# Squares of the delta stage's queries and keys split into high and low parts, two units at a time

## The chip, the cores and the metric

The kernel runs on one core of a Trainium2 chip. The metric is device time in microseconds (us) of one execution, as the median of several runs; a profile is one further execution with the hardware profiler on. TensorE (PE) multiplies matrices, VectorE (DVE) and ScalarE (ACT) work elementwise, GpSimd (POOL) makes constants and issues some loads, SyncE (SP) issues the weight loads.

## The reference

Two layers of a decoder on 256 tokens of 2048 features, all in float32. Layer 0 mixes with a short convolution and a gated DeltaNet of 8 heads, layer 1 with sparse attention; each is followed by a SwiGLU network. The change touches only the norms of queries and keys in the DeltaNet part:

```python
def l2norm(t):
    return t * lax.rsqrt(jnp.sum(jnp.square(t), axis=-1, keepdims=True) + NORM_EPS)

    qkv = jax.nn.silu(causal_depthwise_conv(dn_qkv, dn_conv_w))
    q, k, v = jnp.split(qkv, 3, axis=-1)
    q, k, v, z = l2norm(heads(q)), l2norm(heads(k)), heads(v), heads(dn_z)
```

## The kernel before

**Weights and matmuls.** Every large product is made of three fp32r matmuls on parts: each weight half (128 x 1024 elements, 512 KB) is split into `w_hi`, a rounded copy made by ScalarE (line 681), and `w_lo`, the rest, made by VectorE (line 1192). TensorE multiplies high by high, high by low and low by high (`passes`, lines 1935 to 1937). The parts lie in four slots (`HL_SLOTS`): ScalarE may write half h only when TensorE has used half h - 4 (`half_used`); VectorE follows on `w_hi_ready`, TensorE on `w_lo_ready`. A chunk is eight halves: 512 output columns over all 2048 inputs. In the stage in question the output is by feature, and a half is 24 matmuls of 256 columns. SyncE loads the weights, four slabs of two halves ahead.

**Order.** Each engine runs its own program in order; the order is written out by hand. `halves(n)` in the program of ScalarE or VectorE makes the next n weight parts, so the place of other work among them is fixed.

**The stage around the change.** The six chunks of the short convolution (`sc`, lines 2184 to 2191) run on TensorE while the other engines finish queries, keys and values of the DeltaNet part in `qkvT`. In turn m = 1 to 4 (one per chunk) two units of queries or keys are normalised, eight units in all, each 128 features by 512 values (two heads). ScalarE squares a unit (`square`, line 853), TensorE multiplies the squares by a matrix of ones (`squares_sum`, line 2174), which puts the sum on all partitions, ScalarE takes the root (`norm`, line 860) and VectorE divides (`unit`, lines 1482 and 1483). TensorE's sums stand behind the third half of the chunk for the first unit (2m - 2) and behind the sixth for the second (2m - 1). ScalarE's order in a turn is: square, four halves, root, square, three halves, root, one half, and then the SiLU of the next four heads. VectorE's is: five halves, unit, three halves, unit. Between turns 1 and 2 VectorE multiplies two chunks (line 1503) and runs a convolution (`conv`, lines 1445 and 1447, with one half inside it); turn 2 then starts with four halves instead of five (line 1508). Between turns 2 and 3 stands line 1532, between turns 3 and 4 nothing, and after turn 4 again line 1503 and a convolution, then the decays, whose cumulated sums go out to memory and come back by a broadcast load before the DeltaNet's chunk matrices can be made (line 1541). `norm_sq`, the buffer of the squares, exists once, and so does `norm_q`, that of the roots.

Of the kernel before, what the change touches and what calls it, by code (L numbers as in the profile page):

```python
# [13 lines left out]
F32 = mybir.dt.float32  # L14
F32R = mybir.dt.float32r
I32 = mybir.dt.int32
ALU = mybir.AluOpType
ACT = mybir.ActivationFunctionType
# [3 lines left out]
P = 128  # L22
# [56 lines left out]
def trunk(nc, x_in, positions, ln_mix_g, ln_mix_b, ln_ffn_g, ln_ffn_b, ffn_w_in, ffn_w_out,  # L79
          hy_w_in, sc_conv_w, dn_conv_w, dn_a_log, dn_dt_bias, dn_norm_w, hy_w_out,  # L80
          nsa_w_in, cmp_pos_k, cmp_w1_k, cmp_w2_k, cmp_pos_v, cmp_w1_v, cmp_w2_v, nsa_w_out,
          inv_freq, ln_by_feature, end_positions, x_by_feature, gc_rows, beta_rows, out, stop=None):
# [3 lines left out]
    with ctx:  # L86
        def sem(name):
            return ctx.enter_context(nc.semaphore(name))
# [3 lines left out]
        def sb(name, shape, dt=F32, offset=None):  # L92

            size = 4 * int(np.prod(shape[1:]))
            if offset is None:
                offset = place[0]
                place[0] += (size + 31) // 32 * 32
            return nc.alloc_sbuf_tensor_at(name, shape, dt, offset=offset)
# [13 lines left out]
        big_at = place[0]  # L112
        big = sb("big", [P, 12288])
        yt_at = place[0]
        yt = sb("yt", [P, KT, SEQ])
        gb_at = place[0]
        gb = sb("gb", [P, 2, D])
        ident = sb("ident", [P, P])
        ones = sb("ones", [P, P])
        upper = sb("upper", [P, P])  # L120
        neg_lower = sb("neg_lower", [P, P])
        blk_mask = sb("blk_mask", [P, len(BLOCKS), P])
# [25 lines left out]
        qkvT = part(24 * SEQ, "p (f t) -> p f t", f=24)  # L148
# [35 lines left out]
        conv_in = gb_flat[:, 0:2048].rearrange("p (a f t) -> p a f t", a=2, f=4)  # L184
        conv_out = gb_flat[:, 2048:3072].rearrange("p (f t) -> p f t", f=4)
        ba_out = yt[:, KT - 1, :]
        norm_sq, norm_q = (gb_flat[:, n:n + 512].rearrange("p (h d) -> p h d", h=4) for n in (3072, 3584))

        hT = big[:, 0:FT * SEQ].rearrange("p (f t) -> p f t", f=FT)
        yt_flat = yt[:, :, :].rearrange("p a t -> p (a t)")  # L190
# [67 lines left out]
        gb_in, out_done = sem("gb_in"), sem("out_done")  # L258
        consts, pool_chain, x_scaled = sem("consts"), sem("pool_chain"), sem("x_scaled")
        dve, act_done = sem("dve"), sem("act_done")  # L260
        var_ready, std_ready, nmr_ready, x_normed = sem("var_ready"), sem("std_ready"), sem("nmr_ready"), sem("x_normed")
        xt_hi_ready, xt_lo_ready = sem("xt_hi_ready"), sem("xt_lo_ready")
        stage_free, silu_done = sem("stage_free"), sem("silu_done")
# [105 lines left out]
        for (name, kts), slots in zip(OUTER, SPARES):  # L369
            for p, k in enumerate(slots):  # L370
                if k is not None:
                    h = 2 * (S[name] + kts) - 2 * TAIL + p
# [287 lines left out]
        def _(act):  # L660
            h_next = [0]

            def halves(count, i=None, per=0):

                for _ in range(count):
                    h = h_next[0]
                    if h >= 2 * total_slabs:
                        return
                    if h < 2 * RAW_SLOTS:
                        act.wait_ge((slab_in if h % 2 else first_in)[h // 2], 16)  # L670
                    elif h % 2 == 0:
                        act.wait_ge(slab_in[h // 2 % RAW_SLOTS], at(16 * (h // 2 // RAW_SLOTS + 1), i, 2 * per))
                    if before_in_slot[h] is not None:
                        act.wait_ge(half_used, at(before_in_slot[h] + 1, i, per))
                    if h in all_split:
                        act.wait_ge(a_lo_ready, all_split[h])
                    if h in gates_halves:
                        src = half_of(h).rearrange("p (k n) -> p k n", n=P)[:, :, P - N_GATES:]
                        act.activation(gates_of(h)[:, :, 0:N_GATES], src, ACT.Copy).then_inc(w_hi_ready, 1)
                    else:  # L680
                        act.activation(weights_of(h)[0], half_of(h), ACT.Copy).then_inc(w_hi_ready, 1)  # L681
                    h_next[0] += 1
# [167 lines left out]
                ins.then_inc(from_act, 1)  # L850

            def square(u):
                act.activation(norm_sq, qkvT[:, 2 * u:2 * u + 2, :].rearrange("p f (a t) -> p (f a) t", a=2),
                               ACT.Square).then_inc(act_done, 1)

            def norm(u):
                wait_sp(act, ("norm", u))
# [3 lines left out]
                               ACT.Sqrt, bias=eps_nm[:, :]).then_inc(sp_free[K[("norm", u)] % 4], 1)  # L861

            act.wait_ge(consts, 3)
            soft, expA = sm[:, 9, :], misc_w[:, 120:128]
            for j in range(2):
                for n in range(3):
                    m = 3 * j + n
                    if m == 0:
                        halves(8)
                        wait_sp(act, ("ba",))  # L870
                        act.activation(sm[:, 0:NT, :], last_cols(("ba",), 2 * DNH), ACT.Copy).then_inc(sp_free[K[("ba",)] % 4], 1)
                        done(act.activation(beta_feature, ba_out[P - 32:P, :], ACT.Sigmoid))
                        wait_sp_read(act, ("ba",))
                        done(act.activation(sm[:, 2, :].rearrange("p (t h) -> p t h", t=NT), sm[:, 0:2, 0:8], ACT.Sigmoid))
                    elif m < 5:
                        act.wait_ge(silu_done, m)
                        square(2 * m - 2)
                        halves(4)
                        norm(2 * m - 2)
                        square(2 * m - 1)  # L880
                        halves(3)
                        norm(2 * m - 1)
                        halves(1)
                    else:
                        halves(3)
                        act.wait_ge(for_act, 9)
                        done(act.activation(soft, sm[:, 8, :], ACT.Exp, scale=-1.0))
                        act.wait_ge(from_act, n_from[0])
                        done(act.activation(soft, soft, ACT.Ln, bias=1.0))
                        done(act.activation(expA, expA, ACT.Exp))  # L890
                        halves(3)
                    if n == 0:
                        c = C["sc"] + 3 * j
                        b = chunk_in(c)
                        act.wait_ge(stage_free, 7 + j)
                        for a in range(2):
                            ins = act.activation(conv_in[:, j, 2 * a:2 * a + 2, :],
                                                 b[a][:, :].rearrange("p (f t) -> p f t", f=2), ACT.Copy)
                        ins.then_inc(pair_free[c % 2], 1)

                    act.wait_ge(stage_free, m + 3)
                    act.activation(qkvT[:, 4 * m:4 * m + 4, :], qkvT[:, 4 * m:4 * m + 4, :], ACT.Silu).then_inc(silu_done, 1)
                    if m == 5:
                        act.wait_ge(for_act, 10)
                        done(act.activation(sm[:, 6, :], sm[:, 4, :], ACT.Exp))
                        done(act.activation(sm[:, 14, 8:16], sm[:, 14, 8:16], ACT.Exp))
                        halves(2)
# [159 lines left out]
            name = ("vcmp",)  # L1067
# [80 lines left out]
            v = x[:, 0, FIRST:]  # L1148
# [5 lines left out]
        def _(dv):  # L1154
# [25 lines left out]
            def halves(count, i=None, per=0):  # L1180

                for _ in range(count):
                    h = h_next[0]
                    if h >= 2 * total_slabs:
                        return
                    hi, lo = weights_of(h)
                    src = half_of(h)
                    if h in gates_halves:
                        src = src.rearrange("p (k n) -> p k n", n=P)[:, :, P - N_GATES:]
                        hi, lo = (gates_of(h)[:, :, n * N_GATES:(n + 1) * N_GATES] for n in range(2))  # L1190
                    dv.wait_ge(w_hi_ready, at(h + 1, i, per))
                    dv.tensor_tensor(lo, src, hi.bitcast(F32), ALU.subtract).then_inc(w_lo_ready, 1)  # L1192
                    h_next[0] += 1
# [233 lines left out]
            for p in range(8):  # L1427
                v = slice(2 * p, 2 * p + 2)
# [47 lines left out]
            def unit(u):  # L1476
# [5 lines left out]
                own(dv.reciprocal(r, r))  # L1482
                to_act(dv.scalar_tensor_tensor(v, r, SCALE if u < 4 else 1.0, v, ALU.mult, ALU.mult))

            def halves_and_units(m, first=5):

                halves(first)
                unit(2 * m - 2)
                halves(3)
                unit(2 * m - 1)  # L1490

            for j in range(2):
# [7 lines left out]
                b = chunk_in(c + 1)  # L1500
                for a in range(2):
                    v = conv_in[:, j, 2 * a:2 * a + 2, :].rearrange("p f t -> p (f t)")
# [6 lines left out]
                else:  # L1509
# [8 lines left out]
                    name = ("gc",)  # L1518
                    wait_sp(dv, name)
                    b = sp_bank(name)  # L1520
# [8 lines left out]
                b = chunk_in(c + 2)  # L1529
# [7 lines left out]
            for t, hh in units:  # L1537
                Dt = tiles_of(t, hh)[0]
                for h in range(4):
                    n = 8 * t + 4 * hh + h  # L1540
# [218 lines left out]
            name = ("kcmp",)  # L1759
# [153 lines left out]
        def _(pe):  # L1913
# [9 lines left out]
            def sp_done(ins, name):  # L1923
                ins.then_inc(sp_ready[K[name] % 4], 1)
# [243 lines left out]
            small(S["ba"], C["ba"])  # L2168

            def squares_sum(u):  # L2170
                pe.wait_ge(act_done, u + 1)
                name = ("norm", u)
                b = sp_use(name)
                sp_done(pe.matmul(b[:, :], ones[:, :], norm_sq.rearrange("p h d -> p (h d)"), start=True, stop=True), name)  # L2174

            def decays():

# [385 lines left out]
```

## Time and profile before

| | |
|---|---|
| median of three runs | 2379.5 us (2379.26 to 2380.42) |
| profiled execution | 2381.16 us, of which the span from the first to the last instruction is 2379.4 us |
| TensorE busy | 2345.6 us (99% of the span) |
| VectorE busy | 1558.2 us (65%) |
| ScalarE busy | 1123.7 us (47%) |
| line 2174 (the sums) | 16 matmul records, 592 ns each, two for each of eight units, 185.7 to 269.8 us |
| mean granted TensorE clock | 0.997 of full speed |

Times in the trace are us from the start of the span. A busy TensorE is not TensorE at its peak: matmuls overlap, so what counts is the distance from one start to the next.

### The profile page before, as it was taken

Reading aid. Unit: us, or ns where it says so; the run is one execution under the profiler, and the core shown is the slowest. Engines: PE = TensorE matmul, PEld = TensorE weight load, DVE = VectorE, ACT = ScalarE, POOL = GpSimd, SP = SyncE. Lnnn points to the kernel's source line nnn. Section 1 sums busy time; section 2 is a strip of 40 time slices with the busy share of each in tenths; the row PEclk is TensorE's granted clock in tenths of the full one; section 3 lists DMA queues with packets and bytes.
Section 4 is the critical chain, followed back from the end, with each engine's and each line's share of the span. In section 5 each row is a group of like instructions: output and inputs, shape, how many; then the busy total and the mean of one; then the engine's idle time right before and its main releaser. Section 6 shows DMA issues by size and latency. Waiting matters only on the chain.

```text
span 2379.4 us, 31884 instructions
## 1 busy us (share of the span) xinstructions
PE 2345.6 (99%) x12225; PEld 2008.2 (84%) x12225; DVE 1558.2 (65%) x2097; ACT 1123.7 (47%) x1516; POOL 34.6 (1%) x79
## 2 busy tenths in 40 slices
PE   8999999999999999999999999999999999999998
PEld 8999988888888888888889888888888888888886
DVE  6767776676666666755588657657666666666556
ACT  4346654654444444444465445546444444444443
POOL 1000000100000000000000000000000000000001
PEclk9999999999999999999999999999999999999999
DMA  7555441745555555655547643245555555565553
GB/s 268 184 188 185 166 146 64 300 152 194 193 195 194 194 189 194 227 192 192 192 173 236 227 145 107 89 160 195 177 195 194 194 194 194 194 217 204 191 191 115
DMA packets 180441, 440.08 MB, mean 185 GB/s; under 512 B 7304, under 2 KB 19728, under 8 KB 166016
## 3 DMA queue, kind: packets, MB, share of 16 engines
q1 hardware_dynamic: 177984, 425.75, 51.3%
q0 software_dynamic: 2368, 13.13, 1.4%
q8 instruction: 58, 0.95, 0.2%
q14 instruction: 31, 0.25, 0.0%
HBM read 436.74 MB, written 2.11 MB: 184 GB/s over the span
## 4 chain that ended last, share of the span: by engine, by line
PE 92%; DVE 3%; ACT 3%; issue 1%; DMA 1%; ACTq 0%; DVEq 0%
PE bank L1935 29%; PE bank L1937 29%; PE bank L1936 29%; PE bank L2228 2%; DVE w_lo L1192 1%; PE bank L2431 1%; PE bank L2458 1%; PE bank L2200 1%; ACT w_hi L681 1%; ACT yt L756 1%; DMA dn_more<-gc_rows_dram 0%; PE bank L2449 0%; PE bank L2422 0%; ACT xt_hi L767 0%; PE bank L2174 0%
## 5 line engine op out<-in xcount | busy, mean ns | idle before, releaser
L1192 DVE TENSOR_TENSOR w_lo<-raw,w_hi 128x1024 fp32r<-128x1024 f32 x768 | 933.8, 1224 | 707.5 <-ACT w_hi L681 704.6
L681 ACT ACTIVATE w_hi<-raw 128x1024 fp32r<-128x1024 f32 x768 | 810.3, 1060 | 1049.7 <-PE bank L1937 1035.3
L1935 PE MATMUL bank<-w_hi,xt_hi 128*128 128x512 f32 x1888 | 740.5, 392 | 1.4 <-DVE xt_lo L1222 0.7
L1937 PE MATMUL bank<-w_hi,xt_lo 128*128 128x512 f32 x1888 | 735.7, 390 | 0.0
L1936 PE MATMUL bank<-w_lo,xt_hi 128*128 128x512 f32 x1888 | 735.5, 390 | 0.0
L1935 PEld LDWEIGHTS bank<-w_hi,xt_hi 128*128 128x128 f32 x1888 | 355.1, 188 | 75.0 <-issue 3.1
L1937 PEld LDWEIGHTS bank<-w_hi,xt_lo 128*128 128x128 f32 x1888 | 354.8, 188 | 74.4
L1936 PEld LDWEIGHTS bank<-w_lo,xt_hi 128*128 128x128 f32 x1888 | 355.1, 188 | 72.1
L1935 PE MATMUL bank<-xt_hi,w_hi 128*128 128x256 f32 x912 | 262.4, 288 | 8.5 <-DVE xt_lo L1430 8.2
L1936 PE MATMUL bank<-xt_lo,w_hi 128*128 128x256 f32 x912 | 258.7, 284 | 0.0
L1937 PE MATMUL bank<-xt_hi,w_lo 128*128 128x256 f32 x912 | 258.7, 284 | 0.0
L1935 PE MATMUL bank<-w_hi,a_hi 128*128 128x512 f32 x664 | 258.3, 389 | 0.0
L1936 PE MATMUL bank<-w_lo,a_hi 128*128 128x512 f32 x664 | 258.3, 389 | 0.0
L1937 PE MATMUL bank<-w_hi,a_lo 128*128 128x512 f32 x664 | 258.3, 389 | 0.0
L1935 PEld LDWEIGHTS bank<-xt_hi,w_hi 128*128 128x128 f32 x912 | 175.7, 193 | 10.8 <-DVE xt_lo L1430 8.2
L1936 PEld LDWEIGHTS bank<-xt_lo,w_hi 128*128 128x128 f32 x912 | 175.7, 193 | 2.0 <-issue 1.9
L1937 PEld LDWEIGHTS bank<-xt_hi,w_lo 128*128 128x128 f32 x912 | 175.7, 193 | 0.0
L1399 DVE STREAM_TRANSPOSE big<-yt 32x256 f32<-32x256 f32 x352 | 153.4, 436 | 10.0
L1935 PEld LDWEIGHTS bank<-w_hi,a_hi 128*128 128x128 f32 x664 | 124.6, 188 | 26.1
L1936 PEld LDWEIGHTS bank<-w_lo,a_hi 128*128 128x128 f32 x664 | 124.6, 188 | 25.9
L1937 PEld LDWEIGHTS bank<-w_hi,a_lo 128*128 128x128 f32 x664 | 124.6, 188 | 25.7
L1192 DVE TENSOR_TENSOR spare_lo<-raw,spare_hi 128x1024 fp32r<-128x1024 f32 x34 | 39.7, 1220 | 3.3 <-ACT spare_hi L681 3.3
(290 smaller groups left out, 1489.9 us busy)
## 6 DMA issues: line engine op xcount, KB each, us to landing
raw<-in_ffn_w_in_dram SPq DMA_DIRECT2D x176, 1024.0 KB, 4.8
raw<-in_ffn_w_out_dram SPq DMA_DIRECT2D x88, 1024.0 KB, 4.9
raw<-in_hy_w_in_dram SPq DMA_DIRECT2D x53, 1024.0 KB, 5.0
raw<-in_nsa_w_in_dram SPq DMA_DIRECT2D x41, 1024.0 KB, 5.1
raw<-in_hy_w_out_dram SPq DMA_DIRECT2D x16, 1024.0 KB, 5.2
raw<-in_nsa_w_out_dram SPq DMA_DIRECT2D x16, 1024.0 KB, 5.1
raw<-in_hy_w_in_dram SPq DMA_DIRECT2D x8, 512.0 KB, 8.1
raw<-in_cmp_w_k_dram SPq DMA_DIRECT2D x4, 1024.0 KB, 5.5
```

The lines of the kernel that those rows point to most:

```text
L681: act.activation(weights_of(h)[0], half_of(h), ACT.Copy).then_inc(w_hi_ready, 1)
L756: ins = act.activation(yt[:, kt, tok], src[:, a * P:(a + 1) * P], ACT.Identity, bias=lnT[:, 1, kt:kt + 1], scale=lnT[:, 0, kt:kt + 1])
L1192: dv.tensor_tensor(lo, src, hi.bitcast(F32), ALU.subtract).then_inc(w_lo_ready, 1)
L1399: ins = dv.transpose(dst, src)
L1935: pe.matmul(dst, l_hi, r_hi, start=start, stop=False, skip_group_check=shared)
L1936: pe.matmul(dst, l_hi, r_lo, start=False, stop=False, skip_group_check=shared)
L1937: return pe.matmul(dst, l_lo, r_hi, start=False, stop=stop, skip_group_check=shared)
L2200: ins = pe.transpose(b[0:rows, h * P:(h + 1) * P], src, ident[:, :])
L2228: ins = pe.matmul(b[:, h * P:(h + 1) * P], lhs(h), rhs(h), start=True, stop=True)
L2431: ins = pe.matmul(b[:, h * kn:(h + 1) * kn], qT[:, 4 * g + hp * k + h, v], ksT[:, br, g, 0:kn], start=True, stop=True)
L2458: ins = pe.matmul(b[:, h * P:(h + 1) * P], pT_buf[br][:, k, h * P:(h + 1) * P], vs[:, br, k, g * DH:(g + 1) * DH], start=k == 0, stop=k == t)
```

## The change

Each unit is squared twice by ScalarE, once in float32 into a plain buffer and once rounded to fp32r (`norm_hi`). VectorE subtracts the two (`square_lo`), which gives the rest (`norm_lo`). TensorE adds both parts with two fp32r matmuls against an fp32r copy of the ones, and waits for the low part (`square_lo_ready`) where it waited for the square. There are two sets of buffers, one for each unit of a chunk, so ScalarE squares both units ahead of the turn's first four halves. VectorE makes the first low part after two of the turn's halves (after one in turn 2, where one half has already gone into the convolution) and the second one half later. The new buffers lie in space that other stages use.

```diff
+        ones_r = sb("ones_r", [P, P], F32R)
...
+        norm_hi, norm_lo = ([sb(f"norm_{part_}{k}", [P, 512], F32R, offset=big_at + 4 * (8192 + 1024 * n + 512 * k)) for k in range(2)]
+                            for n, part_ in enumerate(("hi", "lo")))
...
+        norm_sqs = [norm_sq.rearrange("p h d -> p (h d)"), yt[:, 8:10, :].rearrange("p f t -> p (f t)")]
...
             def square(u):
-                act.activation(norm_sq, qkvT[:, 2 * u:2 * u + 2, :].rearrange("p f (a t) -> p (f a) t", a=2),
-                               ACT.Square).then_inc(act_done, 1)
+                v = qkvT[:, 2 * u:2 * u + 2, :].rearrange("p f t -> p (f t)")
+                act.activation(norm_sqs[u % 2], v, ACT.Square)
+                act.activation(norm_hi[u % 2][:, :], v, ACT.Square).then_inc(act_done, 1)
...
             act.wait_ge(consts, 3)
+            act.activation(ones_r[:, :], ones[:, :], ACT.Copy)
...
                         square(2 * m - 2)
+                        square(2 * m - 1)
                         halves(4)
                         norm(2 * m - 2)
-                        square(2 * m - 1)
                         halves(3)
...
+            def square_lo(u):
+
+                dv.wait_ge(act_done, u + 1)
+                dv.tensor_tensor(norm_lo[u % 2][:, :], norm_sqs[u % 2], norm_hi[u % 2][:, :].bitcast(F32), ALU.subtract)\
+                  .then_inc(square_lo_ready, 1)
+
             def halves_and_units(m, first=5):
 
-                halves(first)
+                halves(first - 3)
+                square_lo(2 * m - 2)
+                halves(1)
+                square_lo(2 * m - 1)
+                halves(2)
                 unit(2 * m - 2)
...
             def squares_sum(u):
-                pe.wait_ge(act_done, u + 1)
+                pe.wait_ge(square_lo_ready, u + 1)
                 name = ("norm", u)
                 b = sp_use(name)
-                sp_done(pe.matmul(b[:, :], ones[:, :], norm_sq.rearrange("p h d -> p (h d)"), start=True, stop=True), name)
+                pe.matmul(b[:, :], ones_r[:, :], norm_hi[u % 2][:, :], start=True, stop=False)
+                sp_done(pe.matmul(b[:, :], ones_r[:, :], norm_lo[u % 2][:, :], start=False, stop=True), name)
```

## Rows read from the trace of the kernel before

**Rows 1.** the page: busy time by engine; the chain that ended last.

```profile
PE 2345.6 (99%) x12225; PEld 2008.2 (84%) x12225; DVE 1558.2 (65%) x2097; ACT 1123.7 (47%) x1516; POOL 34.6 (1%) x79
...
PE 92%; DVE 3%; ACT 3%; issue 1%; DMA 1%; ACTq 0%; DVEq 0%
```

**Rows 2.** TensorE in time (start us, us, engine, line, op, operands), units 0, 2, 4, 6.

```profile
185.55 0.28 PE L1937 MATMUL bank<-xt_hi,w_lo 128*128 128x256 f32 x1
185.67 1.02 PE L2174 MATMUL bank<-gb,ones 128*128 128x512 f32 x2
...
186.65 0.28 PE L1936 MATMUL bank<-xt_lo,w_hi 128*128 128x256 f32 x1
...
210.40 1.02 PE L2174 MATMUL bank<-gb,ones 128*128 128x512 f32 x2
...
235.14 1.02 PE L2174 MATMUL bank<-gb,ones 128*128 128x512 f32 x2
...
259.87 1.02 PE L2174 MATMUL bank<-gb,ones 128*128 128x512 f32 x2
```

**Rows 3.** TensorE in time, fp32r matmuls of 512 columns.

```profile
302.16 0.39 PE L1936 MATMUL bank<-w_lo,xt_hi 128*128 128x512 f32 x1
302.39 0.39 PE L1937 MATMUL bank<-w_hi,xt_lo 128*128 128x512 f32 x1
```

**Rows 4.** ScalarE in time, before and at unit 0.

```profile
174.41 1.06 ACT L681 ACTIVATE w_hi<-raw 128x1024 fp32r<-128x1024 f32 x1 [1.88 <-PE bank L1937]
...
180.90 0.63 ACT L853 ACTIVATE gb<-big 128x512 f32<-128x512 f32 x1
181.43 2.94 ACT L681 ACTIVATE w_hi<-raw 128x1024 fp32r<-128x1024 f32 x3
```

**Rows 5.** VectorE in time, at unit 0.

```profile
182.51 3.50 DVE L1192 TENSOR_TENSOR w_lo<-raw,w_hi 128x1024 fp32r<-128x1024 f32 x3 [5.78 <-ACT w_hi L681]
```

**Rows 6.** line 1302, a low part of 512 elements: ns min/median/max of all.

```profile
L1302 DVE TENSOR_TENSOR xt_lo<-yt,xt_hi x24: 627/684/693, 490.5 to 1663.8; 128x512 fp32r<-128x512 f32 x24
```

**Rows 7.** VectorE in time, before unit 2.

```profile
200.24 1.23 DVE L1192 TENSOR_TENSOR w_lo<-raw,w_hi 128x1024 fp32r<-128x1024 f32 x1 [2.07 <-ACT w_hi L681]
...
212.29 4.62 DVE L1192 TENSOR_TENSOR w_lo<-raw,w_hi 128x1024 fp32r<-128x1024 f32 x4
```

**Rows 8.** VectorE in time, before units 4 and 6.

```profile
231.30 3.49 DVE L1192 TENSOR_TENSOR w_lo<-raw,w_hi 128x1024 fp32r<-128x1024 f32 x3
...
256.53 3.50 DVE L1192 TENSOR_TENSOR w_lo<-raw,w_hi 128x1024 fp32r<-128x1024 f32 x3 [1.61 <-ACT w_hi L681]
```

**Rows 9.** VectorE and TensorE in time, at a short wait.

```profile
283.77 1.23 DVE L1192 TENSOR_TENSOR w_lo<-raw,w_hi 128x1024 fp32r<-128x1024 f32 x1
...
285.05 0.38 PE L1935 MATMUL bank<-xt_hi,w_hi 128*128 128x256 f32 x1 [0.29 <-DVE w_lo L1192]
285.27 0.28 PE L1936 MATMUL bank<-xt_lo,w_hi 128*128 128x256 f32 x1
```

**Rows 10.** waits of TensorE, 310 to 318 and 1526 to 1531 (us, times, longest).

```profile
PE bank L2228 <- DVE gb L1569: 2.4, 1, 2.4
...
PE bank L2200 <- ACT big L912: 1.2, 1, 1.2
```

**Rows 11.** busy us (instructions) of PE, PEld, DVE, ACT, POOL; TensorE clock; DMA.

```profile
314.00:316.00 2.00, 1.10 (x7) 1.10 (x8) 1.97 (x4) 0.38 (x2) 0.00 (x0) 0.84 0.87 262
316.00:318.00 2.00, 2.00 (x12) 2.00 (x11) 1.97 (x4) 1.91 (x4) 0.00 (x0) 0.50 0.69 266
318.00:320.00 2.00, 2.00 (x9) 1.68 (x9) 1.97 (x5) 0.59 (x2) 0.00 (x0) 0.81 0.34 76
```

**Rows 12.** TensorE in time, start of the kernel.

```profile
8.80 0.41 PE L1937 MATMUL bank<-xt_hi,w_lo 128*128 128x256 f32 x1
9.02 0.41 PE L1935 MATMUL bank<-xt_hi,w_hi 128*128 128x256 f32 x1
```

**Rows 13.** the chain that ended last, in time, 270 to 300.

```profile
273.34 1.07 ACT w_hi L681
```

More of the change, by code:

```diff
@@ L260, in trunk @@
         dve, act_done = sem("dve"), sem("act_done")
+        square_lo_ready = sem("square_lo_ready")
         var_ready, std_ready, nmr_ready, x_normed = sem("var_ready"), sem("std_ready"), sem("nmr_ready"), sem("x_normed")
```

## The prediction, made before the changed kernel ran

> **What bounds the kernel now.** I read the page first. TensorE is busy for 99% of the span and holds 92% of the chain that ended last [rows 1], so a saving or a wait on TensorE reaches the end unless a later step of another engine takes it back. Then I read TensorE in order of time around line 2174, the sum of squares of one unit. It is due after the third half of its chunk (units 0, 2, 4, 6) and after the sixth (1, 3, 5, 7). From unit 0 at 185.67 to unit 2 at 210.40 lie eight halves and two sums [rows 2]. Matmuls of 256 columns start 0.12 us apart, 24 of them to a half, which is 2.88 us. No row shows TensorE waiting at line 2174: the squares lay ready each time.
>
> Third, I read ScalarE and VectorE over the same stretch. Both run in program order. They make the weight parts, `w_hi` on ScalarE and `w_lo` on VectorE, and are held back by TensorE through four slots, so they mostly wait for it: ScalarE 1.88 us before the half at 174.41 [rows 4], VectorE 2.07 us before the one at 200.24 [rows 7]. What is to be seen in those rows is where, in VectorE's order, the new low part of the squares comes, and when TensorE asks for it. Last, the tail: from 273.34 on the chain leaves TensorE for a weight half of ScalarE, the last unit, a convolution and the decays [rows 13], and then to a load that everything behind waits for. That chain starts with a half that waits for a slot which TensorE frees after the last sum of squares, so whatever TensorE gained or lost up to there moves the whole tail, and everything behind it, by as much.
>
> **What TensorE saves.** An fp32 sum shows as two matmul records. Between its start at 185.67 and the second matmul after it at 186.65 lie 0.98 us, of which one ordinary step is 0.12; so a sum costs 0.86 us of the stream [rows 2]. It is replaced by two fp32r matmuls of 512 columns. The row nearest to these is the fp32r stream of the same width, 0.23 us from start to start (302.16, 302.39) [rows 3], so 0.45 for both. Saved: 8 x (0.86 - 0.45) = 3.3 us. The bounds are no saving (0.86 for the new pair) and the 0.24 of two 256-column steps, which would save 5.0; I take the row of the same shape and type. The Trainium skill ("TensorE: Matmul & The Clock Gate", "Back-to-back issue gap") gives about 131 ns a matmul for sustained streams of 512 columns; by that estimate the pair would cost 0.26 us and the saving would be 4.8 us, but the rows here measure 0.23 us each for the same form, so the measurement decides.
>
> **What ScalarE adds.** One copy of the ones, before its first half of the short-convolution stage: at most one more small activation in a place where it then waits 1 to 2 us for TensorE before each half [rows 4], so nothing. Per unit it writes the square twice, and both units of a chunk are squared ahead of the chunk's first four halves. A 512-element square occupies 0.53 us (180.90 to 181.43) [rows 4]. So where one square stood ahead of those halves there are now four, and the halves start 3 x 0.53 = 1.59 us later. Queued behind them are the three `w_hi` that ScalarE issues without a pause at 181.43, and the root of the first unit, which waits for TensorE anyway. The square that stood between the root and the next half is gone.
>
> **What VectorE adds.** Per unit one subtraction of 512 elements into fp32r. Line 1302 is exactly that form: 0.684 us, of which about 0.07 overlaps the next instruction [rows 6]; eight are 4.9 us of VectorE. It waits for the squares of its unit, which have long been there. Queued behind it are weight halves; the slack on them is one to three halves, so TensorE does not wait for weights. The cost lies elsewhere: TensorE now waits for VectorE at the sum, and in VectorE's order the low part of the chunk's first unit stands behind two weight halves, and behind all that precedes them. TensorE's matmuls go in order, so the weight halves that lie ready cannot be worked on meanwhile. I work out each unit with a step of 1.14 us per `w_lo` (three in 3.50) [rows 5], 0.68 for the subtraction and 0.05 until TensorE starts (the wait that ends at 285.05 follows a `w_lo` of 283.77 + 1.23 = 285.00) [rows 9].
> - Unit 0: `w_lo` started at 182.51 [rows 5], now 1.59 later, 184.10; two of them to 186.38; the low part to 187.06; TensorE goes on at 187.11. It was due at 185.67 [rows 2]: a wait of 1.4 us.
> - Unit 2: VectorE comes here from the half at 200.24, unit 1, the product and the convolution, without a pause, to a run of four `w_lo` at 212.29 [rows 7]. The first of these and the half inside the convolution are the two ahead of the low part: 212.29 + 1.14 + 0.68 + 0.05 = 214.16, and TensorE is due at 210.40 [rows 2]: 3.8 us. This whole piece hangs on a slot that TensorE freed before, so earlier shifts do not change the difference.
> - Unit 4: 231.30 + 2.28 + 0.68 + 0.05 = 234.31 [rows 8] against 235.14 [rows 2]: ready 0.8 us early, nothing.
> - Unit 6: as unit 0, 256.53 + 1.59 + 2.28 + 0.73 = 261.13 [rows 8] against 259.87 [rows 2]: 1.3 us.
> - Units 1, 3, 5, 7 are due three halves (8.6 us) later, and their low part stands one half behind the other: nothing.
>
> Each wait also breaks the stream: after the wait at 285.05 the next matmul came 0.22 us on where 0.12 is usual [rows 9], 0.1 us for each of three. Waits: 1.4 + 3.8 + 1.3 + 0.3 = 6.8 us.
>
> **The clock.** The trace shows the granted clock at 2.4 GHz nearly everywhere, and two falls to 1.2 GHz inside the kernel. One came as TensorE had waited 2.4 us in one piece, the other in a thinner piece with a wait of 1.2 us in it [rows 10]; the stretches behind the first show down to 0.50 [rows 11]. The wait of 3.8 us at unit 2 is longer than either, so I count one fall behind it. Matmuls of 256 columns start 0.22 us apart at the low clock (8.80, 9.02) [rows 12] against 0.12. From 314 to 320 the stretches show 0.84, 0.50 and 0.81 [rows 11], which makes (0.32 + 1.00 + 0.38) / 0.5 = 3.4 us at the low clock. If all of that falls on work, it costs 3.4 x (1 - 0.12 / 0.21) = 1.5 us; if part of it still lies in the wait, about 0.9; if it stays low for twice as long, up to 3. I take 1.4, near the fall after the single wait, in which nearly all was work. The waits of 1.4 and 1.3 us stand alone and are shorter than what preceded either fall, so I count none there. [...]
>
> **The sum.** -3.3 + 6.8 + 1.4 = +4.9 us. No step further on absorbs it: VectorE's own additions end in its waits, such as the 2.07 us before the chunk's eighth half [rows 7], and the tail starts from TensorE [rows 13]. The profiled execution took 2381.2 us, 1.8 beyond its span of 2379.4; the median of the runs is 2379.5, so I add to that: 2384.4 us (a profiled execution of about 2386). A measurement of this kernel can tell about 0.2%, 4.8 us, from no change; the forecast stands just beyond that.
>
> **The rivals.**
> - *The clock holds.* Everything as above without the fall: +3.5, 2383.0. For it: the slow stretches of the trace follow work that is also thinner in matmuls (transposes, small fp32 products), where here the stream is dense up to the wait. Against it: 3.8 us is half again the longest wait that preceded a fall.
> - *More falls, or no cheaper pair.* Falls also behind units 0 and 6, 1.4 each, make 2387.2; a pair of fp32r matmuls as dear as the fp32 one makes 2387.7. Against the first: the short waits; against the second: rows 3.
> - *No wait for the low parts: not slower.* One mechanism, on VectorE: if its low part were ready by the time TensorE asks at unit 2 and the two short waits vanished as well, only the saving is left, 2376.2, which is no difference either. It decides at unit 2: for the whole change to come out at nothing the waits and the fall together must stay below 3.3 us, so the low part there must be ready about 3 us sooner, before the convolution and not behind it. For it speaks only that VectorE is idle a third of the kernel. Against it: the half at 200.24 comes 2 us after a pause, but the run at 212.29 has none marked before it [rows 7]; VectorE works through from one to the other.
> - That the change doesn't do what it says would be an fp32r pair that runs like the fp32 one, the second half of the case above.
>
> **How the numbers follow.** Forecast, waits and one fall: 0.60, own range 2383.3 to 2386.0, which straddles the 0.2% bound at 2384.3, a little more than half of it above. Clock holds: 0.19. More falls or dear pair: 0.14. No waits: 0.07. So slower by over 0.2% has 0.36 + 0.14 = 0.50, within 0.2% the rest of the forecast, the held clock and nearly all of the last case, 0.48; faster by over 0.2% needs 4.8 us saved, which only the cheapest bound for the pair and no wait would give: 0.02. The range is 2381.5 to 2387.2: below, the held clock with 1.5 us less waiting; above, two more falls.
>
> **What would show it right or wrong.** At line 2174's successor the trace should show two fp32r matmuls 0.23 us apart, and TensorE idle until VectorE's new subtraction about 1.4, 3.8, 0 and 1.3 us at units 0, 2, 4, 6. VectorE's time between its half before unit 1 and the low part of unit 2 should be as long as now. The clock should show a low stretch just behind unit 2 and none at units 0 and 6. The kernel's end should move by what TensorE has lost by the time of unit 7. The forecast is wrong if the wait at unit 2 is below 2 us, if the pair costs over 0.6 us, or if TensorE waits for weights in this stage.

## The result, and the profile after

The changed kernel takes 2386.17 us (median of nine runs, 2382.61 to 2388.1), the kernel before 2379.86 in the same job (nine runs). The ratio is 1.0025 with a 95% interval of 1.0017 to 1.0034, so it is slower by a quarter of a per cent, 6.3 us by the medians. The forecast was 2384.4 with a range of 2381.5 to 2387.2 and 0.50 for slower by over 0.2%.

| | before | after |
|---|---|---|
| profiled execution | 2381.16 us | 2387.61 us |
| its span | 2379.4 us | 2385.2 us |
| TensorE busy | 2345.6 us | 2345.2 us |
| VectorE busy | 1558.2 us | 1563.2 us |
| ScalarE busy | 1123.7 us | 1127.7 us |
| table load for the sigmoid (line 872, 880) to the decays' first matmul | 175.6 to 293.9, 118.3 us | 176.7 to 301.2, 124.5 us |
| the decays' matmul to the first product of line 1569 (1587) | 20.3 us | 20.0 us |
| from there to the last of line 1666 (1684) | 109.5 us | 108.4 us |
| from there to the end of the span | 1955.7 us | 1955.6 us |

The page answers [rows 1] with nearly the same busy times. TensorE's idle time, the span less the busy time, grew from 33.8 to 40.0 us, but the totals do not tell where:

```profile
span 2385.2 us, 31900 instructions
...
PE 2345.2 (98%) x12225; PEld 2010.2 (84%) x12225; DVE 1563.2 (66%) x2105; ACT 1127.7 (47%) x1525; POOL 34.4 (1%) x79
```

All of it is in the 120 us of the short convolution's chunks. These are TensorE's waits there, 176 to 300 us:

```profile
PE bank L2192 <- DVE norm_lo L1496: 5.9, 3, 3.6
PE bank L1953 <- DVE w_lo L1200: 0.3, 1, 0.3
```

TensorE in order of time at units 0, 2, 4 and 6, which answers [rows 2]. The step of 0.12 us to the sum's start is exceeded by 1.41 us at unit 0 (186.65 to 188.18), by 3.75 at unit 2 and by 1.24 at unit 6. At unit 4 there is no wait, and the pair takes from 242.65 to 243.12, 0.47 us; behind the wait at unit 0 it takes 0.58 (188.18 to 188.76), which is the restart of 0.1 us:

```profile
186.65 0.28 PE L1955 MATMUL bank<-xt_hi,w_lo 128*128 128x256 f32 x1
188.18 0.50 PE L2192 MATMUL bank<-norm_hi,ones_r 128*128 128x512 f32 x1 [1.25 <-DVE norm_lo L1496]
188.52 0.40 PE L2193 MATMUL bank<-norm_lo,ones_r 128*128 128x512 f32 x1
188.76 0.28 PE L1953 MATMUL bank<-xt_hi,w_hi 128*128 128x256 f32 x1
...
212.12 0.28 PE L1955 MATMUL bank<-xt_hi,w_lo 128*128 128x256 f32 x1
215.99 0.80 PE L2192 MATMUL bank<-norm_hi,ones_r 128*128 128x512 f32 x1 [3.60 <-DVE norm_lo L1496]
216.59 0.63 PE L2193 MATMUL bank<-norm_lo,ones_r 128*128 128x512 f32 x1
217.01 0.41 PE L1953 MATMUL bank<-xt_hi,w_hi 128*128 128x256 f32 x1
217.23 0.41 PE L1954 MATMUL bank<-xt_lo,w_hi 128*128 128x256 f32 x1
...
242.53 0.28 PE L1955 MATMUL bank<-xt_hi,w_lo 128*128 128x256 f32 x1
242.65 0.40 PE L2192 MATMUL bank<-norm_hi,ones_r 128*128 128x512 f32 x1
242.88 0.40 PE L2193 MATMUL bank<-norm_lo,ones_r 128*128 128x512 f32 x1
243.12 0.28 PE L1953 MATMUL bank<-xt_hi,w_hi 128*128 128x256 f32 x1
...
266.46 0.28 PE L1955 MATMUL bank<-xt_hi,w_lo 128*128 128x256 f32 x1
267.82 0.50 PE L2192 MATMUL bank<-norm_hi,ones_r 128*128 128x512 f32 x1 [1.08 <-DVE norm_lo L1496]
```

VectorE at units 0 and 2 answers [rows 5, 7]. The low part (line 1496) ends at 187.44 + 0.68 = 188.12 and at 215.25 + 0.69 = 215.94, each time 0.05 or 0.06 us before TensorE starts. Between 211.40 and 215.25 VectorE has no idle time: the rest of the convolution and two weight halves stand in front.

```profile
185.16 2.36 DVE L1200 TENSOR_TENSOR w_lo<-raw,w_hi 128x1024 fp32r<-128x1024 f32 x2 [7.33 <-ACT w_hi L687]
187.44 0.68 DVE L1496 TENSOR_TENSOR norm_lo<-gb,norm_hi 128x512 fp32r<-128x512 f32 x1
...
211.40 1.22 DVE L1200 TENSOR_TENSOR w_lo<-raw,w_hi 128x1024 fp32r<-128x1024 f32 x1
212.54 1.66 DVE L1455 SCALAR_TENSOR_TENSOR gb<-gb,misc_w 128x254 f32<-128x254 f32 x4
214.12 1.22 DVE L1200 TENSOR_TENSOR w_lo<-raw,w_hi 128x1024 fp32r<-128x1024 f32 x1
215.25 0.69 DVE L1496 TENSOR_TENSOR norm_lo<-gb,norm_hi 128x512 fp32r<-128x512 f32 x1
```

The clock, in stretches of two us and columns as in [rows 11]: it is low from within 214 to 216 until 222. The shares add up to 6.8 us at the low clock; the fall comes some 0.9 us before the wait at unit 2 ends, so that 5.9 us of it lie on work. From 316 to 324 it stays high, where the kernel before had its first fall.

```profile
212.00:214.00 2.00, 0.40 (x4) 0.20 (x2) 2.00 (x5) 1.49 (x2) 0.00 (x0) 1.00 0.14 20
214.00:216.00 2.00, 0.01 (x1) 0.01 (x1) 2.00 (x4) 0.85 (x1) 0.00 (x0) 0.77 0.96 328
216.00:218.00 2.00, 2.00 (x7) 1.81 (x8) 2.00 (x3) 0.69 (x1) 0.00 (x0) 0.50 0.46 176
218.00:220.00 2.00, 2.00 (x11) 2.00 (x10) 0.81 (x1) 0.00 (x0) 0.00 (x0) 0.50 0.85 256
220.00:222.00 2.00, 2.00 (x11) 2.00 (x11) 0.00 (x0) 0.00 (x0) 0.00 (x0) 0.52 0.69 268
222.00:224.00 2.00, 2.00 (x19) 2.00 (x18) 0.67 (x1) 1.06 (x1) 0.00 (x0) 1.00 0.00 0
316.00:320.00 4.00, 3.76 (x22) 2.94 (x20) 3.97 (x13) 2.74 (x5) 0.00 (x0) 1.00 0.00 0
320.00:324.00 4.00, 1.92 (x14) 1.73 (x15) 3.93 (x7) 1.73 (x6) 0.00 (x0) 1.00 0.69 225
```

In the stage the parts add up: eight pairs at 0.47 for 0.86 save 3.1; the waits cost 1.4 + 3.75 + 1.25 = 6.4 and 0.3 for three restarts; the low clock costs 2.6 (the pair at unit 2 1.02 for 0.58, and 23 steps of 0.21 for 0.12). That is +6.2, and the stage shows 124.5 - 118.3 = +6.2. Outside it, the start was 1.1 us later in this execution, and this was not the change: TensorE's matmuls at the start of the kernel stood 0.21 us apart until 13.7 us here and until 11.6 in the profile of the kernel before. The missing fall near 316 gave 1.1 back, and 0.3 came from the stretch before it, so that the span grew by 5.8.

### The profile page after: what moved, and what is told of

The parts are those of the page before. It is cut to its first block, busy times and chain, and to the rows that moved or that the text cites. A ratio compares the mean times of both kernels' runs of the same rounds, so it can differ in the third digit from the quotient of the medians.

```text
span 2385.2 us, 31900 instructions
## 1 busy us (share of the span) xinstructions
PE 2345.2 (98%) x12225; PEld 2010.2 (84%) x12225; DVE 1563.2 (66%) x2105; ACT 1127.7 (47%) x1525; POOL 34.4 (1%) x79
## 4 chain that ended last, share of the span: by engine, by line
PE 91%; DVE 4%; ACT 4%; issue 1%; DMA 1%; ACTq 0%; DVEq 0%
PE bank L1953 28%; PE bank L1955 28%; PE bank L1954 28%; PE bank L2247 1%; DVE w_lo L1200 1%; PE bank L2450 1%; ACT w_hi L687 1%; PE bank L2477 1%; PE bank L2219 1%; ACT yt L762 1%; DMA dn_more<-gc_rows_dram 0%; PE bank L2468 0%; PE bank L2441 0%; ACT xt_hi L773 0%; DVE gb L1490 0%
```

## The experiments

Two theories. *Order*: the sum waits for a low part that stands too late in VectorE's order, and the longest of these waits lowers the clock; the work itself costs nothing. *Work*: the added instructions of VectorE and ScalarE cost wherever they stand. Beside them: whether the pair is really cheaper, and what the clock costs. "The stage" below is the stretch of the table above, 118.3 us before and 124.5 after, read from the trace of each kernel in the same way. It is sharper than the runs, whose intervals are some 2 us to either side. It is read from one execution each, but where kernels do the same work in it, it repeats: 118.3 us in the kernel before and in the two with unused semaphores below, 124.5 in the changed kernel and in the one without its semaphore.

### The low parts first

```diff
 def halves_and_units(m, first=5):
-    halves(first - 3)
-    square_lo(2 * m - 2)
-    halves(1)
-    square_lo(2 * m - 1)
-    halves(2)
+    if first == 5:
+        square_lo(2 * m - 2)
+        square_lo(2 * m - 1)
+    halves(first)
...
+if j == 0:
+    square_lo(2)
+    square_lo(3)
 c = C["sc"] + 3 * j
 chunk_staged(c)
```

> Edit to the changed kernel: VectorE makes both low parts of a turn ahead of the turn's first weight half, for turn 2 ahead of line 1503's product and the convolution. Theory of order (TensorE loses 6.5 us waiting for low parts that stand too late in VectorE's order, and the clock falls behind the longest of these waits): no wait at the sums, no fall of the clock behind unit 2, and only the cheaper pair is left, 3.3 us faster than the kernel before, about 9 us faster than the changed kernel. Theory of work (VectorE's eight subtractions, 4.9 us, and ScalarE's second squares cost wherever they stand): as slow as the changed kernel, some 6 us slower than before.

2378.45 us against 2379.94 of the kernel before, ratio 0.9994 (0.9985 to 1.0003); the stage 116.4 us, 1.9 less than before and 8.1 less than the changed kernel's. All work is still there, and the clock does not fall behind unit 2, so the theory of work falls. But 1.2 us of the 3.1 that the pair saves are missing, and the trace says where. The sum at unit 2 no longer waits, but the next weight half does, because the two low parts now stand ahead of the convolution that holds its low part (211.17 + 1.23 = 212.40, TensorE at 212.45). TensorE in order of time, and last that weight half on VectorE:

```profile
210.81 0.40 PE L2194 MATMUL bank<-norm_hi,ones_r 128*128 128x512 f32 x1
211.04 0.40 PE L2195 MATMUL bank<-norm_lo,ones_r 128*128 128x512 f32 x1
212.45 0.39 PE L1955 MATMUL bank<-xt_hi,w_hi 128*128 128x256 f32 x1 [1.02 <-DVE w_lo L1200]
...
211.17 1.23 DVE L1200 TENSOR_TENSOR w_lo<-raw,w_hi 128x1024 fp32r<-128x1024 f32 x1
```

### Only unit 2

```diff
-    square_lo(2 * m - 2)
+    if m != 2:
+        square_lo(2 * m - 2)
...
+if j == 0:
+    square_lo(2)
 c = C["sc"] + 3 * j
```

> Edit to the changed kernel: only the low part of unit 2 moves, ahead of line 1503's product and the convolution. Theory of order: the wait at unit 2 goes, 3.8 us, and the clock's fall behind it, 1.5 to 2.5 us; the waits of 1.4 and 1.3 us at units 0 and 6 stay: about 0.4 us faster than the kernel before, within what can be told from none. No low clock between 210 and 225 us in the trace. Theory of work: about 6 us slower than before.

2381.4 us, ratio 1.0004 (0.9995 to 1.0013). The stage took 118.7 us: 5.8 less than the changed kernel's, and 0.4 more than before, where 0.4 less was expected. A wait for weights at unit 2, as above, makes up 0.6 us of the difference, and two restarts that the expectation left out 0.2. One low part moved gives back 5.8 of 6.2 us, the wait and the low clock behind it together: the clock stays high from 210 to 225 us, as expected. TensorE's waits, 176 to 300:

```profile
PE bank L2195 <- DVE norm_lo L1496: 2.3, 2, 1.3
PE bank L1956 <- DVE w_lo L1200: 0.7, 2, 0.4
```

### The fp32 sum with the waits kept

```diff
-pe.matmul(b[:, :], ones_r[:, :], norm_hi[u % 2][:, :], start=True, stop=False)
-sp_done(pe.matmul(b[:, :], ones_r[:, :], norm_lo[u % 2][:, :], start=False, stop=True), name)
+sp_done(pe.matmul(b[:, :], ones[:, :], norm_sqs[u % 2], start=True, stop=True), name)
```

> Edit to the changed kernel: TensorE sums the plain float32 squares in one fp32 matmul again, but still waits for the low part. If the fp32r pair saves 0.41 us a unit: 3.3 us slower than the changed kernel, 9 to 10 us slower than before. If the pair is no cheaper in this place: the time of the changed kernel, about 6 us slower than before.

2388.96 us, ratio 1.0040 (1.0026 to 1.0053), 9.0 us above the kernel before of the same job, where the changed kernel was 6.3 above its own; the stage 126.6 us, 2.1 above the changed kernel's, in an execution whose clock was low for half as long behind unit 2 (about 3.4 us, where the changed kernel's profile has 6.8). The dearer sums cost 3.1 us and the shorter fall about 1.1 less (1.5 for 2.6), which leaves 2.0 of the 2.1: the pair is cheaper also amid the waits.

### The pair alone

```diff
...
-act.activation(norm_sq, qkvT[:, 2 * u:2 * u + 2, :].rearrange("p f (a t) -> p (f a) t", a=2),
-               ACT.Square).then_inc(act_done, 1)
+act.activation(norm_hi[:, :], qkvT[:, 2 * u:2 * u + 2, :].rearrange("p f t -> p (f t)"),
+               ACT.Square).then_inc(act_done, 1)
...
-sp_done(pe.matmul(b[:, :], ones[:, :], norm_sq.rearrange("p h d -> p (h d)"), start=True, stop=True), name)
+pe.matmul(b[:, :], ones_r[:, :], norm_hi[:, :], start=True, stop=False)
+sp_done(pe.matmul(b[:, :], ones_r[:, :], norm_hi[:, :], start=False, stop=True), name)
```

> Edit to the kernel before: ScalarE writes the squares rounded to fp32r, TensorE sums them in two fp32r matmuls, both of the high part; the low part is left out, so the norms are off. ScalarE's and VectorE's order stay as before. If the pair's saving of 0.39 us a unit reaches the end: 3.1 us faster than before. If it is taken back on the way (by VectorE, or by weights that are not ready): no difference.

2377.22 us against 2380.12, ratio 0.9988 (0.9979 to 0.9997); the stage 115.2 us, 3.1 less than before, to the tenth what 8 x 0.39 gives. The saving passes through to the end of the stage in full.

### The work alone

```diff
-pe.wait_ge(square_lo_ready, u + 1)
+pe.wait_ge(act_done, u + 1)
...
-pe.matmul(b[:, :], ones_r[:, :], norm_hi[u % 2][:, :], start=True, stop=False)
-sp_done(pe.matmul(b[:, :], ones_r[:, :], norm_lo[u % 2][:, :], start=False, stop=True), name)
+sp_done(pe.matmul(b[:, :], ones[:, :], norm_sqs[u % 2], start=True, stop=True), name)
```

> Edit to the changed kernel: ScalarE and VectorE do all that they do there, in the same order, but TensorE sums the plain float32 squares in one fp32 matmul and waits for the squares alone, so nobody waits for the low parts. Theory of order: no difference from the kernel before, 0 to 1 us slower. Theory of work: some 5 us slower, VectorE's 4.9 us.

2381.16 us, ratio 1.0006 (0.9997 to 1.0015), and the stage 118.3 us, exactly that of the kernel before. Seventeen more instructions, nine on ScalarE and eight on VectorE, all but one of 512 elements, cost the path nothing. Of the 1.0 us in the medians 0.6 lie outside the span (see the semaphores below).

### The sum one half later

```diff
-after = {3: lambda: squares_sum(2 * n - 2), 6: lambda: squares_sum(2 * n - 1)}
+after = {4: lambda: squares_sum(2 * n - 2), 6: lambda: squares_sum(2 * n - 1)}
```

> Edit to the changed kernel: TensorE takes the first sum of each chunk behind the fourth half and not the third, 2.9 us later. VectorE's and ScalarE's programs stay. Theory of order: the waits at units 0 and 6 vanish, that at unit 2 shrinks from 3.8 to about 0.9 us and brings no fall of the clock; about 2.3 us faster than the kernel before. Theory of work: as the changed kernel, some 6 us slower than before.

2379.03 us, ratio 0.9996 (0.9987 to 1.0005); the stage 116.1 us, 2.2 less than before, where 2.3 was expected. One digit in TensorE's program does the same as moving VectorE's work. The wait at unit 2 is 0.3 us and not 0.9, since TensorE had already waited 0.4 for the weight half before it; with a restart behind each they make the 0.9.

### The wait filled with matmuls

```diff
-pe.wait_ge(square_lo_ready, u + 1)
 name = ("norm", u)
 b = sp_use(name)
+if u == 2:
+    pe.wait_ge(act_done, u + 1)
+    for _ in range(14):
+        pe.matmul(b[:, :], ones_r[:, :], norm_hi[u % 2][:, :], start=True, stop=True)
+pe.wait_ge(square_lo_ready, u + 1)
```

> Edit to the changed kernel: while TensorE waits for the low part of unit 2, it runs 14 fp32r matmuls of 512 columns on the high part (3.2 of the 3.8 us); the sum overwrites them, so they only keep it busy. If the low clock behind unit 2 is a price of its own, beside the wait: the trace shows no low clock there, and the kernel is 1.5 to 2.5 us faster than the changed one, though TensorE does more; about 3.7 us slower than before. If the fall costs nothing on the path: the time of the changed kernel, some 6 us slower than before.

The sum starts as late as in the changed kernel (215.93), but the clock holds, and the stage takes 121.9 us, 2.6 less than the changed kernel's and 3.6 more than before, as the parts without the clock give (6.4 + 0.3 - 3.1):

```profile
212.00:216.00 4.00, 3.61 (x18) 2.69 (x17) 4.00 (x8) 2.35 (x2) 0.00 (x0) 1.00 0.55 153
216.00:220.00 4.00, 4.00 (x32) 3.91 (x33) 2.74 (x3) 1.13 (x2) 0.00 (x0) 1.00 0.71 222
220.00:224.00 4.00, 4.00 (x35) 4.00 (x35) 3.35 (x2) 1.68 (x2) 0.00 (x0) 1.00 0.63 187
```

The runs show less of it: 2385.1 us, ratio 1.0021 (1.0012 to 1.0030), 1.1 us below the changed kernel's median, and the two intervals overlap. So in one execution of each the low clock is shown as a price of 2.6 us of its own; how much it is on average is not settled, about 1 us by the medians. Three profiles have the full wait of 3.75 us: the changed kernel's and that of the same kernel without its semaphore (below) were at the low clock for 6.8 us behind it, that of the fp32 sum for 3.4. The changed kernel's own runs vary too: the six with a mean clock of 0.997 took 2386.0 to 2388.1 us, the three with 0.998 took 2382.6 to 2384.0. But that mean takes in the clock of the whole kernel, and two other falls come and go (last section), so it does not say which fall was missing.

### Sums and weights both moved, and a last version

```diff
-after = {3: lambda: squares_sum(2 * n - 2), 6: lambda: squares_sum(2 * n - 1)}
+after = {5 if n == 2 else 4: lambda: squares_sum(2 * n - 2), 6: lambda: squares_sum(2 * n - 1)}
...
-if tap == 1:
+if tap == (1 if taps == DNK else 0):
     halves(1, i, per_halves)
```

> Edit to the changed kernel: the first sum of a chunk stands behind the fourth half (behind the fifth in turn 2), and VectorE makes the weight half inside the short convolution one tap earlier, so that neither the sums nor the weights are waited for. Theory of order: the saving alone, 3.1 us faster than before, 9 us faster than the changed kernel. If moved sums hold up roots and units, and through them the tail: less than 2 us faster than before.

2378.53 us, ratio 0.9994 (0.9985 to 1.0003); the stage 115.5 us, 2.8 less than before. TensorE now waits 0.3 us at 213.7 for the second weight half of that turn, and has the restart of 0.1 behind it. The last version puts this half into the convolution too, and counts the low parts on `base_in_ready` in place of a semaphore of their own; the first sums stay behind the fourth half, in turn 2 the fifth:

```diff
...
-if tap == 1:
+if tap in halves_at:
     halves(1, i, per_halves)
...
-conv(conv_out, conv_in[:, j, :, :], lambda f, tap: ..., SCK)
+conv(conv_out, conv_in[:, j, :, :], lambda f, tap: ..., SCK,
+     halves_at=(1,) if j else (0, 1))
...
-halves_and_units(2, 4)
+halves_and_units(2, 3)
...
-  .then_inc(square_lo_ready, 1)
+  .then_inc(base_in_ready, 1)
...
-dv.wait_ge(base_in_ready, 1)
+dv.wait_ge(base_in_ready, 9)
...
-pe.wait_ge(square_lo_ready, u + 1)
+pe.wait_ge(base_in_ready, u + 1)
...
```

> Edit to the changed kernel: first sums behind the fourth half (the fifth in turn 2), both weight halves ahead of unit 2's low part drawn into the short convolution of turns 1 to 2, and no new semaphore. Theory of order: no wait of TensorE at the sums or for weights in turns 1 to 4, so the saving alone, 3.1 us faster than before; with the old number of semaphores nothing is lost outside the span.

2378.08 us against 2380.35, ratio 0.9992 (0.9983 to 1.0001); the stage 115.1 us, 3.2 less than before, all that the pair can give. In the four turns nothing is waited for; the one wait left lies in the tail, as before:

```profile
PE bank L1953 <- DVE w_lo L1199: 0.3, 1, 0.3
```

By the medians, each against the kernel before of its own job, it is 8.6 us better than the changed kernel and 2.3 better than the one before. The interval just includes no difference, so that this last gain rests on the stage in the trace.

### Semaphores and the time outside the span

All runs of the kernel before took 1.7 to 1.8 us beyond the span, those of the changed kernel 2.3 on average. The pair alone, which has no new semaphore, took 1.7. Hence three more kernels: one and four unused semaphores added to the kernel before,

```diff
 dve, act_done = sem("dve"), sem("act_done")
+unused = sem("unused")
```

```diff
 dve, act_done = sem("dve"), sem("act_done")
+unused = [sem(f"unused{n}") for n in range(4)]
```

> Edit to the kernel before: one more semaphore is allocated, which nobody uses. All kernels so far with the semaphore square_lo_ready took some 2.3 us beyond their span, those without it 1.7. If the semaphore itself is the cause: 0.6 us slower than before, all of it outside the span. If the cause is a use of it, or other code of the change: no difference, 1.7 us beyond the span.

> Edit to the kernel before: four more unused semaphores. If each semaphore costs alike: 2.3 us more outside the span, 4 us in all beyond it. If a step is crossed once (as a group is full): 0.6 us more, as with one. If neither: 1.7 us beyond the span.

and the changed kernel without its own (as in the last diff above, with nothing else moved):

> Edit to the changed kernel: the low parts are signalled on base_in_ready, a semaphore that is used only later for one wait, and square_lo_ready is gone. If the semaphore is the cause of the time beyond the span: back to 1.7 us beyond it, 0.6 us faster than the changed kernel, about 5.7 us slower than before. If not: the changed kernel's time and 2.3 us beyond its span.

The unused ones: 2380.64 us (ratio 1.0002, 0.9993 to 1.0011) and 2380.44 (1.0001, 0.9992 to 1.0010), both 1.7 beyond the span. The changed kernel without the new semaphore: 2386.53 (1.0028, 1.0017 to 1.0039), 2.4 beyond it, its stage 124.5. So the semaphore is not the cause. The expectation of the last version, that nothing is lost outside the span, missed as well: it has 2.3. What in the changed kernel adds 0.6 us outside the span stays open. The ten kernels with it all have the low parts and the second set of buffers, the four without (before, the pair alone, the unused semaphores) have neither; the copy of the ones is not it, since the pair alone has that.

## Why the prediction held, step by step

- *What TensorE saves*: 0.45 us for a pair was 0.47, and 3.3 in all was 3.1, passed on in full (the pair alone). The 131 ns a matmul that the Trainium skill gives for sustained streams of 512 columns ("TensorE: Matmul & The Clock Gate", "Back-to-back issue gap") were not met: 0.23 to 0.24 us each here, as in [rows 3].
- *What ScalarE and VectorE add*: nothing on the path, as said; shown by the work alone, with its stage of 118.3 us. VectorE takes as long from its half before unit 1 to the half before unit 2's low part as it did (202.08 to 214.12, before 200.24 to 212.29).
- *The waits*: forecast 1.4, 3.8, 0 and 1.3 us, measured 1.41, 3.75, 0 and 1.24. Following one engine's program step by step from the slot that starts it, with steps read from rows, was good to 0.1 us. The odd units waited for nothing.
- *The restart*: 0.1 us each, as [rows 9] had it.
- *The clock*: the fall came where forecast and at the longest wait alone. Its size was the term mis-sized in the profile: 1.4 us put down, 2.6 found, since the clock stayed low for 6.8 us and not 3.4. The prediction had named this case (up to 3 us) as a bound. Of three profiles with the same waits two had 6.8 us of it and one 3.4, so 1.4 is one of its values and not the mean.
- *A reading that does not hold*: the waits of 1.4 and 1.3 us are not shorter than what preceded either fall, since the second fall followed a wait of 1.2 [rows 10] and one of 0.7 us. That no fall came behind them was right; the row that speaks for it, and that the prediction did not use, is a wait of 1.4 us of the kernel before, with one of 0.4 near it, that no fall followed (waits of TensorE, 1430 to 1440):

```profile
PE bank L2200 <- DVE sm L1173: 1.4, 1, 1.4
```

- *The sum*: +4.9 was +6.3. The stage without the clock was forecast at +3.5 and is +3.6 (the filled wait). Outside the span lie 0.6 us, which no step of the prediction had: it took the 1.8 us beyond the span as fixed. That leaves 2.1 us for the clock by the medians, where 1.4 was put down. The forecast time of 2384.4 lies 1.8 below the 2386.17; 0.4 of this is that it was added to the 2379.5 of three runs, where nine gave 2379.86. The result is in the range by the room left for the clock; that the 0.6 us also found room in it is luck.
- *The rivals*: the clock did not hold; it fell once, not thrice; the pair was cheaper; and the waits were there. The decisive condition named for the rival on the other side, a low part ready before the convolution, is the edit that gave back 5.8 us. With that edit alone the stage came out 0.4 us above the kernel before.
- *Not foreseen*: that moving the low part ahead of the convolution makes TensorE wait for the weight half inside it, 1.2 us (with both low parts) and 0.6 (with one). With the cheap pair and the sum moved behind the next half it was late by 0.4 even with VectorE's order unchanged. The old sum, 0.86 us long and in front of that half, had probably covered part of it; no run isolates this.

## What to carry to other kernels

Making a step cheaper on the bounding engine can add a new handoff to it; cost the handoff by following the giving engine's program, in its order, to the point where the taking engine asks, since how busy either is says nothing (VectorE was at 65%). If it comes too late, move the question before moving the answer: asking one piece of work later cost 0.9 us here, and nothing with the weight halves moved too, where answering earlier pushed other work that was just in time. And a wait of 3.75 us on TensorE cost more than its length here in all three profiles that have it, as the clock was low behind it.

## What the runs showed of the hardware

- Around the end of a wait of 3.75 us TensorE went to 1.2 GHz in all three profiles that have this wait: for 6.8 us in two (the changed kernel's, and the one without its semaphore), for 3.4 in one (the fp32 sum). Filled with 14 matmuls whose results are thrown away, the same wait left the clock at 2.4 GHz in the one profile of it.
- Behind the single waits of 1.2 to 1.4 us at units 0 and 6 no fall came in any of the five profiles that have them.
- Whether a shorter wait brings a fall varies from one execution to the next. Near 316 us all fourteen profiles have a wait of 1.8 to 2.5 us. Eight show a fall there, behind waits of 1.8 to 2.5, and six show none, behind waits of 1.8 to 2.2: the changed kernel's, those of the fp32 sum, the pair alone and the changed kernel without its semaphore, and both with unused semaphores, which are the kernel before in all they execute. From the first of line 1569 to the last of line 1666 the eight take 109.5 to 110.0 us and the six 108.3 to 108.5.
- Near 1530 us, behind waits of 1.2 and 0.7 us, seven of the fourteen show a fall and seven none, and from the last of line 1666 to the end the span is 1955.6 to 1955.8 us with it and 1954.0 to 1954.1 without. So two falls outside the stage go with a difference of some 1.4 and 1.6 us between single executions, as much as some of the differences that these experiments look for. The stage leaves both out; the whole span and the median do not.
- Semaphores that are only allocated cost nothing that these runs can tell, one or four.
